# Column sums of the modulation vectors in a two-block transformer kernel: ones products replaced by transposes and ScalarE sums

## The chip, the core and the metric

The kernel runs on one core of a Trainium2 chip. The core has a matrix engine (TensorE, PE in the profile, with its weight loads shown apart as PEld), two engines that work on 128 partitions at once (VectorE, DVE; ScalarE, ACT), GpSimd (POOL) and SyncE (SP), which here only issue transfers, and 16 DMA engines. The metric is the time of one execution on the device in microseconds (us). The kernel before takes 2347.35 us, the median of three runs (2347.17 to 2348.92).

## What is computed

Two transformer blocks follow each other on 256 rows of 2048 columns, all in float32. What matters here is the second block's modulation: two vectors of 2048 values (one for the rows, one for the context) go through a SiLU and a 2048 x 12288 matrix, and the six resulting vectors (shifts SH1 and SH2, scales SC1 and SC2, gates GT1 and GT2) modulate the normalised rows.

```python
mx = jax.nn.silu(c) @ w_mod[i] + b_mod[i]
mc = jax.nn.silu(c_ctx) @ w_mod[i] + b_mod[i]
sh1, sc1, gt1, sh2, sc2, gt2 = [t[:, None, :] for t in jnp.split(mx, 6, axis=-1)]
sh1c, sc1c, gt1c, sh2c, sc2c, gt2c = jnp.split(mc, 6, axis=-1)
hc = modulate(rmsnorm(ctx, norm1_g[i]), sh1c, sc1c)      # h * (1 + scale) + shift
hx = modulate(rmsnorm(x, norm1_g[i]), sh1, sc1)
```

Of the context's six vectors only SH1 and SC1 are needed.

## The kernel before

**The large products.** Every weight matrix is read in groups of 512 rows x 512 columns (1 MB, two pieces of 256 rows). For each piece ScalarE rounds the float32 weights to a short form (`whi`, L486, `round_groups`), VectorE forms the remainder (`wlo`, L919, `remainders`), and TensorE multiplies three times: short times short, remainder times short, short times remainder (L1516 to L1518, `multiply`). A group is 24 products of 128x512. `whi` and `wlo` hold two groups, so ScalarE and VectorE work two groups ahead of TensorE: ScalarE rounds a piece of group g+2 as soon as TensorE has finished that piece of group g (semaphore `piece_multiplied`), VectorE follows it (`hi_done`), TensorE waits for `lo_done`. The product of four groups stands in one of two pairs of PSUM banks and is then taken out by ScalarE (`proj`, L595; `relu_square`) or added to the rows by VectorE (`add_block`, L1124).

**The modulation beside them.** The matrix `w_mod` is not multiplied on TensorE. GpSimd loads it in 192 steps of 256 rows x 512 columns into the two slots of `mring`, and VectorE adds the rows, each scaled by its value of `csil`, into `macc` (`mod_steps`, L935 and L939), two instructions of 128x512 a step, or four where the context is wanted too ("dual": SH1, SC1). After eight steps `macc` holds, for 512 columns, 128 partial sums, one in each partition. TensorE sums them over the partitions (`reduce_mod`, L1541): one product per 128 columns with `macc` as weights and a column of ones, four for a single vector, eight for a dual one, into `m1`. VectorE then adds the bias and writes `modT` (`set_mod`, L948), and only after that starts the next eight steps, which overwrite `macc`.

**When.** There are 24 such reductions: four of SH1 (dual) beside the first block's input projection and the start of its output projection; in each of the four chunks of the first block's MLP (32 groups, `mlp_chunk`) one of SC2, SC1 (dual), GT1 and SH2, after groups 7, 15, 22 and 30 (`MLP_REDUCED`); and four of GT2 in the second block's input projection (`in_blocks`). The order on each engine is the order in which its code is written; loops over chunks and pairs of blocks repeat it.

**Other users of the banks.** `m0` also takes the unused output of ScalarE's squares (`square`, L520), from which the norms come. At the end of a chunk VectorE adds block 3 (L1124, `h_added`), and ScalarE squares it; in the first chunk ScalarE squares the context instead, and both engines then scale it (L1006 to L1020, L549).

Of the kernel before, what the change touches and what calls it, by code (L numbers as in the profile page):

```python
# [108 lines left out]
def two_blocks(nc, x, ctx_in, w_in, w_fourier, w_out, w_up, w_down, w_mod, w_in2, w_out2, w_gate,  # L109
               w_up2, w_down2, vectors, gates_w, mid_g, final_g, tables, fourier_tables, attn_tables, out):  # L110
    ctx = ExitStack()
    with ctx:
# [24 lines left out]
        modT = sb("modT", [P, 2, 6 * KT])  # L137
        gain1 = sb("gain1", [P, 2, KT])
# [78 lines left out]
        mod_reduced = sem("mod_reduced")  # L217
        mod_set = sem("mod_set")
# [257 lines left out]
        def _(act):  # L476
# [37 lines left out]

            def square(src, col, piece, junk=m0):

                for t in range(T):
                    if c.n.get("ssq", 0):
                        act.wait_ge(ssq_done, c.at("ssq"))
                    act.activation(junk[:, :], src[:, t, bass.ds(col, NB)], ACT.Square,  # L520
                                   accum_out=squares[:, t, bass.ds(piece, 1)]).then_inc(ssq_done, 1)
                    c.add("ssq")
# [55 lines left out]
            def w_in_pair(i, first=False):  # L578
                for j in range(2):
# [17 lines left out]
                    last.then_inc(proj_set, 1)  # L597

# [6 lines left out]
            with c.loop(act, 4, 1, g=8) as i:  # L605
# [55 lines left out]
            for n in range(3):  # L661
                round_groups(4)
# [27 lines left out]
            def mlp_chunk(first=False, last=False):  # L690

                def round_group(g):
                    round_groups(1)
                    if last and g in CTX_TURNS:
# [20 lines left out]
            with c.loop(act, MLP_CHUNKS - 1, 1, g=32, q=8, half=4, blk=4, ha=4, ssq=4 * T):  # L715
# [193 lines left out]
        def _(dve):  # L909
# [33 lines left out]

            def set_mod(kind, i, dual):

                dve.wait_ge(mod_reduced, c.at("mb", 1))
                for who in range(2 if dual else 1):
                    dve.tensor_tensor(modT[:, who, bass.ds(i * 4 + kind * KT, 4)], m1[:, 4 * who:4 * who + 4],  # L948
                                      vecs[:, 1, bass.ds(i * 4 + kind * KT, 4)], ALU.add).then_inc(mod_set, 1)
# [89 lines left out]
            def w_in_pair(i, first=False):  # L1039

                for g in range(8):
# [10 lines left out]
                    elif not first and g == 1:  # L1052
                        mod_steps(1, 7, True)
                        remainders(1)
                        set_mod(SH1, i - 1, True)
                    elif g != 1:
                        remainders(1)
                    if g >= 2:
# [15 lines left out]
            with c.loop(dve, 4, 1, g=8, m=8, ma=32, mb=1) as i:  # L1074
# [45 lines left out]
            set_mod(SH1, 3, True)  # L1120
# [11 lines left out]
            for n in range(4):  # L1132
# [6 lines left out]
                remainders(1)  # L1139
            remain_added(3)  # L1140
# [11 lines left out]
            def mlp_chunk(i, first=False, last=False):  # L1152
                done = 0
                for g in range(32):
# [9 lines left out]
                    if g in MLP_REDUCED:  # L1164
                        set_mod(MLP_REDUCED[g], i, MLP_REDUCED[g] == SC1)
                        if last and MLP_REDUCED[g] == SC1:
# [19 lines left out]
            with c.loop(dve, MLP_CHUNKS - 1, 1, g=32, q=8, hi=8, m=32, ma=80, mb=4) as i:  # L1186
# [107 lines left out]
            def in_blocks(names, p):  # L1294
                for n, name in enumerate(names):
                    following = (names + (("w_out",) if p else ("cc0",)))[n + 1]
                    which, part = MOD_PAIRS[p].get(name, (None, 0))
                    for kg in range(2 if name == "l" else 4):
# [7 lines left out]
                        if which is not None:  # L1306
                            k = 4 * part + kg
                            mod_steps(SPREAD[k], sum(SPREAD[0:k]), False)
                            if k == 7:
                                set_mod(GT2, which, False)  # L1310
# [684 lines left out]
```

## Time and profile before

| what | value |
|---|---|
| three runs, median (lowest to highest) | 2347.35 us (2347.17 to 2348.92) |
| the profiled execution's own time | 2348.28 us |
| its span in the profile | 2346.6 us |
| TensorE busy | 2301.8 us, 98% |
| VectorE, ScalarE busy | 1552.7 us, 1082.0 us |
| moved by DMA | 523.92 MB, mean 223 GB/s |

The profile is of one execution. Times in its rows are counted from the start of the span; "x8" in a row of the timeline means eight instructions that follow each other, with the time from the first one's start to the last one's end. Matrix products overlap, so what one costs is read from the distance between starts, not from its duration. What stands in brackets at a row's end is the idle time of that engine before it and what ended it. A float32 product with ones is recorded as two passes, a transpose and a product of the large matrices as one.

### The profile page before, as it was taken

How to read it: one execution, taken by the hardware profiler on the slowest of the kernel's cores; microseconds unless marked ns; L12 is line 12 of the kernel's file. 1: busy time of each engine (PE TensorE's matmuls, PEld its weight loads, DVE VectorE, ACT ScalarE, POOL GpSimd, SP SyncE). 2: the span in 40 equal slices, each digit the busy share in tenths (PEclk: the TensorE clock that was granted, in tenths of full speed). 3: DMA queues.
4: the chain of work that ended last, by engine and by line, in shares of the span. 5: the costliest groups of instructions: out<-in, count | busy, mean ns of one | idle time of the engine just before them, and what ended most of it. 6: DMA issues, size and time to landing. Idle time of an engine off the chain costs nothing.

```text
span 2346.6 us, 29309 instructions
## 1 busy us (share of the span) xinstructions
PE 2301.8 (98%) x10637; PEld 1894.0 (81%) x10637; DVE 1552.7 (66%) x1845; ACT 1082.0 (46%) x1295; POOL 146.2 (6%) x213
## 2 busy tenths in 40 slices
PE   8999999999999999999999999998999999999997
PEld 7887888888888888888877877787888888888886
DVE  7987558877877877886778664466445544555545
ACT  5445455445444444445463464444444344434444
POOL 1110001111111111110010000000000000000000
PEclk9999999999999999999999999999999999999999
DMA  9884459888887888886677663464555665555553
GB/s 343 292 273 148 128 177 312 294 290 286 269 292 259 267 299 267 269 277 213 224 246 217 202 215 117 154 233 154 187 191 186 208 200 185 196 189 190 196 179 108
DMA packets 245187, 523.92 MB, mean 223 GB/s; under 512 B 20016, under 2 KB 20288, under 8 KB 243776
## 3 DMA queue, kind: packets, MB, share of 16 engines
q1 hardware_dynamic: 213680, 404.80, 52.8%
q0 software_dynamic: 29568, 111.97, 13.8%
q10 hardware_dynamic: 1808, 5.37, 0.6%
q8 instruction: 86, 1.41, 0.2%
q14 instruction: 45, 0.37, 0.0%
HBM read 517.87 MB, written 4.21 MB: 222 GB/s over the span
## 4 chain that ended last, share of the span: by engine, by line
PE 96%; DVE 2%; ACT 1%; issue 1%; DMA 0%; ACTq 0%; DVEq 0%
PE acc L1516 30%; PE acc L1518 29%; PE acc L1517 29%; PE tp L1531 2%; PE m L1541 1%; PE tp L1806 1%; DVE wlo L919 0%; PE acc L1651 0%; PE m L1772 0%; PE tp L1824 0%; PE tp L1818 0%; PE acc L1615 0%; PE tp L1751 0%; PE tp L1762 0%; PE m L1625 0%
## 5 line engine op out<-in xcount | busy, mean ns | idle before, releaser
L919 DVE TENSOR_TENSOR wlo<-wring,whi 128x1024 fp32r<-128x1024 f32 x776 | 935.2, 1214 | 602.7 <-ACT whi L486 599.3
L486 ACT ACTIVATE whi<-wring 128x1024 fp32r<-128x1024 f32 x776 | 813.5, 1051 | 1115.5 <-PE acc L1518 1112.0
L1516 PE MATMUL acc<-whi,xhi 128*128 128x512 f32 x2112 | 833.7, 395 | 2.7 <-issue 1.9
L1518 PE MATMUL acc<-whi,xlo 128*128 128x512 f32 x2112 | 823.9, 390 | 0.0
L1517 PE MATMUL acc<-wlo,xhi 128*128 128x512 f32 x2112 | 823.4, 390 | 0.0
L1516 PEld LDWEIGHTS acc<-whi,xhi 128*128 128x128 f32 x2112 | 397.5, 188 | 95.3 <-issue 14.4
L1518 PEld LDWEIGHTS acc<-whi,xlo 128*128 128x128 f32 x2112 | 397.2, 188 | 84.1
L1517 PEld LDWEIGHTS acc<-wlo,xhi 128*128 128x128 f32 x2112 | 397.8, 188 | 81.0 <-issue 0.7
L939 DVE SCALAR_TENSOR_TENSOR macc<-mring,csil,macc 128x512 f32<-128x512 f32 x480 | 344.2, 747 | 28.0 <-DMA mring<-w_mod 21.2
L1516 PE MATMUL acc<-whi,ahi 128*128 128x512 f32 x608 | 239.1, 393 | 2.6 <-DVE h L1124 1.4
L1518 PE MATMUL acc<-whi,alo 128*128 128x512 f32 x608 | 237.0, 390 | 0.0
L1517 PE MATMUL acc<-wlo,ahi 128*128 128x512 f32 x608 | 236.6, 389 | 0.0
L425 POOL DMA_DIRECT2D mring<-w_mod x192 | 136.4, 711 | 1125.4 <-DVE macc L939 1104.5
L1516 PE MATMUL acc<-whi,bhi 128*128 128x512 f32 x352 | 137.2, 390 | 1.6 <-DVE blo L959 1.6
L1517 PE MATMUL acc<-wlo,bhi 128*128 128x512 f32 x352 | 137.0, 389 | 0.0
L1518 PE MATMUL acc<-whi,blo 128*128 128x512 f32 x352 | 137.0, 389 | 0.0
L1516 PEld LDWEIGHTS acc<-whi,ahi 128*128 128x128 f32 x608 | 114.2, 188 | 26.2 <-issue 3.3
L1518 PEld LDWEIGHTS acc<-whi,alo 128*128 128x128 f32 x608 | 114.1, 188 | 24.2
L1517 PEld LDWEIGHTS acc<-wlo,ahi 128*128 128x128 f32 x608 | 114.2, 188 | 23.0
L1516 PEld LDWEIGHTS acc<-whi,bhi 128*128 128x128 f32 x352 | 66.1, 188 | 15.5 <-DVE blo L959 1.8
L1518 PEld LDWEIGHTS acc<-whi,blo 128*128 128x128 f32 x352 | 66.1, 188 | 13.8
L1517 PEld LDWEIGHTS acc<-wlo,bhi 128*128 128x128 f32 x352 | 66.1, 188 | 13.5
(213 smaller groups left out, 1047.6 us busy)
## 6 DMA issues: line engine op xcount, KB each, us to landing
wring<-w_up SPq DMA_DIRECT2D x216, 512.0 KB, 4.7
wring<-w_down SPq DMA_DIRECT2D x216, 512.0 KB, 5.0
mring<-w_mod POOLq DMA_DIRECT2D x192, 512.0 KB, 5.1
wring<-w_in SPq DMA_DIRECT2D x184, 512.0 KB, 5.5
wring<-w_gate SPq DMA_DIRECT2D x88, 512.0 KB, 4.4
wring<-w_out SPq DMA_DIRECT2D x64, 512.0 KB, 4.8
gbig<-ctx_in POOLq DMA_DIRECT2D x2, 1024.0 KB, 8.5
hspill<-h ACTq DMA_DIRECT2D x1, 2048.0 KB, 7.9
```

What stands on the lines that cost most here:

```text
L425: pool.dma_start(mring[:, c.slot("m", MSLOTS), :, :], w_mod_v[s, :, :, bass.ds(i * NB + kind * D, NB)])\
L486: act.activation(whi[:, piece_slot(c, piece), 0:half], wring[:, g4, piece * half:(piece + 1) * half], ACT.Copy).then_inc(hi_done, 1)
L919: dve.tensor_tensor(wlo[:, h4, 0:half], wring[:, g4, piece * half:(piece + 1) * half], whi[:, h4, 0:half].bitcast(F32), ALU.subtract).then ...
L939: dve.scalar_tensor_tensor(macc[:, who, :], mring[:, m2, kt, :], csil[:, who, k:k + 1], macc[:, who, :], ALU.mult, ALU.add).then_inc(mod_a ...
L1516: pe.matmul(dst, hi[:, tile, rows], whi[:, h4, w], start=(kg == first and k == 0), stop=False)
L1517: pe.matmul(dst, hi[:, tile, rows], wlo[:, h4, w], start=False, stop=False)
L1518: last = pe.matmul(dst, lo[:, tile, rows], whi[:, h4, w], start=False, stop=(kg == final and k == KG - 1))
L1531: last = pe.transpose(tp[:, q, j * S + t * P:j * S + (t + 1) * P], src[:, t, f:f + P], ident)
L1541: last = pe.matmul(m1[:, 4 * who + j:4 * who + j + 1], macc[:, who, j * P:(j + 1) * P], ones[:, 0:1], start=True, stop=True)
L1806: last = pe.matmul(tp[:, (q + bank) % 2, (ck // 2) * DV:(ck // 2 + 1) * DV], kdec[rows, ck // 2, d, hd * DK:(hd + 1) * DK], gv[rows, ck // ...
```

## The change

In 20 of the 24 reductions (SH1, SC2, SC1, GT1, SH2) TensorE no longer multiplies with ones. It transposes each 128x128 part of `macc` against the identity into a bank: `m1` for the rows' vector, `m0` for the context's. ScalarE then reads each 128 columns of the bank, writes them back in place with Copy, and sums them in its accumulator into one column of `modsum` (`sum_mod`). VectorE waits for the transposes before it overwrites `macc` (`take_mod`), and adds the bias from `modsum` one group later (`set_mod`). ScalarE's `square` waits for its own sums, since both write `m0`. The four reductions of GT2 stay as they were, under the names `reduce_gate` and `set_gate`. The tables, the transfers and GpSimd's and SyncE's order are the same.

```diff
@@ tiles and semaphores @@
+        modsum = sb("modsum", [P, 2, KG])
...
+        mod_turned = sem("mod_turned")
+        mod_summed = sem("mod_summed")
@@ ScalarE @@
+            def sum_mod(dual):
+
+                for who in range(2 if dual else 1):
+                    bank = m0 if who else m1
+                    c.add("mt")
+                    act.wait_ge(mod_turned, c.at("mt"))
+                    for j in range(KG):
+                        cols = slice(j * P, (j + 1) * P)
+                        act.activation(bank[:, cols], bank[:, cols], ACT.Copy,
+                                       accum_out=modsum[:, who, j:j + 1]).then_inc(mod_summed, 1)
+
             def square(src, col, piece, junk=m0):
...
+                    if t == 0 and c.n.get("mt", 0):
+                        act.wait_ge(mod_summed, c.at("mt", 0, KG))
...
                     last.then_inc(proj_set, 1)
+                    if not first and j == 0:
+                        sum_mod(True)
...
             for n in range(3):
-                round_groups(4)
+                round_groups(2)
+                if n == 0:
+                    sum_mod(True)
+                round_groups(2)
                 round_added(n)
...
                 def round_group(g):
                     round_groups(1)
+                    if g - 1 in MLP_REDUCED:
+                        sum_mod(MLP_REDUCED[g - 1] == SC1)
@@ VectorE @@
+            def take_mod(dual):
+
+                c.add("mt", 2 if dual else 1)
+                dve.wait_ge(mod_turned, c.at("mt"))
+
             def set_mod(kind, i, dual):
 
+                c.add("msum", KG * (2 if dual else 1))
+                dve.wait_ge(mod_summed, c.at("msum"))
+                for who in range(2 if dual else 1):
+                    dve.tensor_tensor(modT[:, who, bass.ds(i * 4 + kind * KT, 4)], modsum[:, who, :],
+                                      vecs[:, 1, bass.ds(i * 4 + kind * KT, 4)], ALU.add).then_inc(mod_set, 1)
+
+            def set_gate(kind, i):
+
                 dve.wait_ge(mod_reduced, c.at("mb", 1))
-                for who in range(2 if dual else 1):
-                    dve.tensor_tensor(modT[:, who, bass.ds(i * 4 + kind * KT, 4)], m1[:, 4 * who:4 * who + 4],
-                                      vecs[:, 1, bass.ds(i * 4 + kind * KT, 4)], ALU.add).then_inc(mod_set, 1)
+                dve.tensor_tensor(modT[:, 0, bass.ds(i * 4 + kind * KT, 4)], m1[:, 0:4],
+                                  vecs[:, 1, bass.ds(i * 4 + kind * KT, 4)], ALU.add).then_inc(mod_set, 1)
                 c.add("mb")
...
                         mod_steps(1, 7, True)
                         remainders(1)
-                        set_mod(SH1, i - 1, True)
                     elif g != 1:
                         remainders(1)
+                    if not first and g == 2:
+                        take_mod(True)
+                    elif not first and g == 3:
+                        set_mod(SH1, i - 1, True)
                     if g >= 2:
                         mod_steps(1, g - 2, True)
...
-            set_mod(SH1, 3, True)
...
                 add_block(n * NB, n % 2)
                 remainders(1)
+                if n == 0:
+                    take_mod(True)
+                    set_mod(SH1, 3, True)
...
                     if g in MLP_REDUCED:
-                        set_mod(MLP_REDUCED[g], i, MLP_REDUCED[g] == SC1)
-                        if last and MLP_REDUCED[g] == SC1:
+                        take_mod(MLP_REDUCED[g] == SC1)
+                    if g - 1 in MLP_REDUCED:
+                        kind = MLP_REDUCED[g - 1]
+                        set_mod(kind, i, kind == SC1)
+                        if last and kind == SC1:
                             set_gain1()
...
-                                set_mod(GT2, which, False)
+                                set_gate(GT2, which)
@@ TensorE @@
                 pe.wait_ge(mod_acc, c.at("ma", 8))
                 for who in range(2 if dual else 1):
+                    bank = m0 if who else m1
                     for j in range(4):
-                        last = pe.matmul(m1[:, 4 * who + j:4 * who + j + 1], macc[:, who, j * P:(j + 1) * P],
-                                         ones[:, 0:1], start=True, stop=True)
+                        last = pe.transpose(bank[:, j * P:(j + 1) * P], macc[:, who, j * P:(j + 1) * P], ident)
+                    last.then_inc(mod_turned, 1)
+
+            def reduce_gate(per_nb):
+
+                c.add("ma", per_nb)
+                pe.wait_ge(mod_acc, c.at("ma", 8))
+                for j in range(4):
+                    last = pe.matmul(m1[:, j:j + 1], macc[:, 0, j * P:(j + 1) * P], ones[:, 0:1], start=True, stop=True)
                 last.then_inc(mod_reduced, 1)
...
-                        reduce_mod(16, False)
+                        reduce_gate(16)
```

On VectorE, in the loop over pairs of blocks of the input projection, before (L919 makes a remainder `wlo`, L948 writes `modT`):

```order
L919 TENSOR_TENSOR wlo<-wring,whi 128x1024 [waits hi_done]
L918 REGISTER_ALU
L919 TENSOR_TENSOR wlo<-wring,whi 128x1024 [waits hi_done]
L948 ISA [waits mod_reduced]
L948 REGISTER_ALU
L948 TENSOR_TENSOR modT<-m,vecs 128x4
L948 ISA
L948 TENSOR_TENSOR modT<-m,vecs 128x4
L918 REGISTER_ALU
L919 TENSOR_TENSOR wlo<-wring,whi 128x1024 [waits hi_done]
L918 REGISTER_ALU
L919 TENSOR_TENSOR wlo<-wring,whi 128x1024 [waits hi_done]
```

and now (L942 makes a remainder, L962 adds into `macc`, L977 writes `modT`):

```order
L962 SCALAR_TENSOR_TENSOR macc<-mring,csil,macc 128x512 [waits mod_acc]
L941 REGISTER_ALU
L942 TENSOR_TENSOR wlo<-wring,whi 128x1024 [waits hi_done]
L941 REGISTER_ALU
L942 TENSOR_TENSOR wlo<-wring,whi 128x1024 [waits hi_done]
L975 REGISTER_ALU
L977 ISA [waits mod_summed]
L977 REGISTER_ALU
L977 TENSOR_TENSOR modT<-modsum,vecs 128x4
L977 ISA
L977 TENSOR_TENSOR modT<-modsum,vecs 128x4
```

The write of `modT` has moved behind the remainders of one more group, the first step of the next sum (the L962 row at the top is its last instruction) and the remainders of a second group, and waits for ScalarE's sums; ahead of that first step stands a wait for TensorE's transposes (`mod_turned`).

On ScalarE, in the same loop, the two copies of a finished block (`proj`) and the rounding of the next weights (`whi`), before:

```order
L595 ISA [waits piece_multiplied]
L595 ACTIVATE proj<-acc,rstd 128x512
L595 ISA
L595 ACTIVATE proj<-acc,rstd 128x512
L485 REGISTER_ALU [waits piece_landed2_0]
L486 ACTIVATE whi<-wring 128x1024 [waits piece_multiplied]
L485 REGISTER_ALU [waits piece_landed2_1]
```

and now (L526 is a sum):

```order
L611 ISA [waits piece_multiplied]
L611 ACTIVATE proj<-acc,rstd 128x512
L611 ISA
L611 ACTIVATE proj<-acc,rstd 128x512
L523 ISA
L526 ACTIVATE m,modsum<-m 128x128 [waits mod_turned]
L526 ACTIVATE m,modsum<-m 128x128 x3
L526 ACTIVATE m,modsum<-m 128x128 [waits mod_turned]
L526 ACTIVATE m,modsum<-m 128x128 x3
L488 REGISTER_ALU [waits piece_landed2_0]
L489 ACTIVATE whi<-wring 128x1024 [waits piece_multiplied]
```

Eight sums now stand between the copies and the next rounding.

On VectorE at the end of the MLP's first chunk, before (L1124 adds the last block, L1006 to L1020 are the context's norm):

```order
L919 TENSOR_TENSOR wlo<-wring,whi 128x1024 [waits hi_done] x2
L948 TENSOR_TENSOR modT<-m,vecs 128x4 [waits mod_reduced]
L1124 TENSOR_TENSOR h<-acc,h 128x2x512 [waits piece_multiplied]
L919 TENSOR_TENSOR wlo<-wring,whi 128x1024 [waits hi_done] x2
L1006 TENSOR_REDUCE ssq<-squares 128x2 [waits ssq_done]
L1008 TENSOR_SCALAR ssq<-ssq 128x2 [waits squares_summed]
L1014 RECIPROCAL rstd<-ssq 128x2 [waits root_done]
L1020 TENSOR_SCALAR gbig<-gbig,rstd 128x2048 [waits rstd_done]
```

and now:

```order
L942 TENSOR_TENSOR wlo<-wring,whi 128x1024 [waits hi_done] x2
L977 TENSOR_TENSOR modT<-modsum,vecs 128x4 [waits mod_summed,mod_turned]
L1161 TENSOR_TENSOR h<-acc,h 128x2x512 [waits piece_multiplied]
L942 TENSOR_TENSOR wlo<-wring,whi 128x1024 [waits hi_done] x2
L1041 TENSOR_REDUCE ssq<-squares 128x2 [waits ssq_done]
L1043 TENSOR_SCALAR ssq<-ssq 128x2 [waits squares_summed]
L1049 RECIPROCAL rstd<-ssq 128x2 [waits root_done]
L1055 TENSOR_SCALAR gbig<-gbig,rstd 128x2048 [waits rstd_done]
```

No row has moved here; what the write of `modT` waits for has changed. Before it waited for products that TensorE had issued a group earlier, now for sums that ScalarE makes at this place, and the addition of the last block and the remainders of the next group stand behind it.

## Rows read from the trace of the kernel before

**Rows 1.** The page: TensorE's busy time, the chain that ended last, ScalarE's rounding
```profile
PE 2301.8 (98%) x10637; PEld 1894.0 (81%) x10637; DVE 1552.7 (66%) x1845; ACT 1082.0 (46%) x1295; POOL 146.2 (6%) x213
...
PE 96%; DVE 2%; ACT 1%; issue 1%; DMA 0%; ACTq 0%; DVEq 0%
...
L486 ACT ACTIVATE whi<-wring 128x1024 fp32r<-128x1024 f32 x776 | 813.5, 1051 | 1115.5 <-PE acc L1518 1112.0
```

**Rows 2.** Timeline (start us, duration us, engine): first products of two successive groups, TensorE
```profile
889.44 0.39 PE L1516 MATMUL acc<-whi,ahi 128*128 128x512 f32 x1
...
894.88 0.39 PE L1516 MATMUL acc<-whi,ahi 128*128 128x512 f32 x1
```

**Rows 3.** TensorE timeline: a dual reduction, then a single one, between products
```profile
121.55 0.39 PE L1518 MATMUL acc<-whi,xlo 128*128 128x512 f32 x1
121.78 1.84 PE L1541 MATMUL m<-ones,macc 128*128 128x1 f32 x16
123.48 0.49 PE L1516 MATMUL acc<-whi,xhi 128*128 128x512 f32 x1
...
384.74 0.39 PE L1518 MATMUL acc<-whi,alo 128*128 128x512 f32 x1
...
385.78 0.49 PE L1516 MATMUL acc<-whi,ahi 128*128 128x512 f32 x1
```

**Rows 4.** TensorE timeline: eight transposes, then four, between products
```profile
372.94 0.40 PE L1518 MATMUL acc<-whi,alo 128*128 128x512 f32 x1
373.17 1.04 PE L1531 MATMUL tp<-tabs,blk 128*128 128x128 f32 x8
373.96 0.47 PE L1516 MATMUL acc<-whi,ahi 128*128 128x512 f32 x1
...
1009.85 0.40 PE L1518 MATMUL acc<-whi,xlo 128*128 128x512 f32 x1
...
1010.44 0.48 PE L1516 MATMUL acc<-whi,xhi 128*128 128x512 f32 x1
```

**Rows 5.** The products with ones by form: busy us, mean ns, idle before
```profile
L1541 PE MATMUL m<-ones,macc 128*128 128x1 f32 x256 | 30.0, 242 | 0.0
```

**Rows 6.** ScalarE timeline: accumulating ACTIVATEs and what starts behind them
```profile
1421.57 0.38 ACT L791 ACTIVATE tmpT<-tp 128x256 f32<-128x256 f32 x1
...
1421.93 0.39 ACT L790 ACTIVATE h<-tp 128x256 f32<-128x256 f32 x1
...
890.98 0.60 ACT L520 ACTIVATE m<-h 128x512 f32<-128x512 f32 x1 [0.28 <-DVE h L1124]
...
891.74 0.60 ACT L520 ACTIVATE m<-h 128x512 f32<-128x512 f32 x1
```

**Rows 7.** Timelines of VectorE, ScalarE, TensorE behind the second SH1 reduction
```profile
123.88 0.30 DVE L948 TENSOR_TENSOR modT<-m,vecs 128x4 f32 x2 [2.45 <-PE m L1541]
130.36 1.23 DVE L919 TENSOR_TENSOR wlo<-wring,whi 128x1024 fp32r<-128x1024 f32 x1 [0.62 <-ACT whi L486]
131.50 2.73 DVE L939 SCALAR_TENSOR_TENSOR macc<-mring,csil,macc 128x512 f32<-128x512 f32 x4
...
130.23 1.25 ACT L595 ACTIVATE proj<-acc,rstd 128x512 f32 x2
...
139.94 0.39 PE L1516 MATMUL acc<-whi,xhi 128*128 128x512 f32 x1
```

**Rows 8.** ScalarE and VectorE timelines at the end of the third chunk
```profile
889.64 1.06 ACT L486 ACTIVATE whi<-wring 128x1024 fp32r<-128x1024 f32 x1 [1.66 <-PE acc L1518]
...
889.64 1.23 DVE L1124 TENSOR_TENSOR h<-acc,h 128x1024 f32<-128x1024 f32 x1 [4.01 <-PE acc L1518]
890.78 2.35 DVE L919 TENSOR_TENSOR wlo<-wring,whi 128x1024 fp32r<-128x1024 f32 x2
```

**Rows 9.** Timelines at the end of the first chunk: VectorE, then TensorE
```profile
523.14 1.22 DVE L1124 TENSOR_TENSOR h<-acc,h 128x1024 f32<-128x1024 f32 x1 [3.95 <-PE acc L1518]
530.36 2.36 DVE L919 TENSOR_TENSOR wlo<-wring,whi 128x1024 fp32r<-128x1024 f32 x2 [1.70 <-ACT whi L486]
...
533.82 0.39 PE L1516 MATMUL acc<-whi,ahi 128*128 128x512 f32 x1
```

**Rows 10.** Busy us of each engine in a window, granted clock of TensorE (PEclk)
```profile
372.00:376.00 4.00, 4.00 (x23) 3.37 (x22) 3.39 (x5) 2.03 (x3) 1.26 (x2) 1.00 0.81 250
1500.00:1503.50 3.50, 3.50 (x10) 2.79 (x9) 2.23 (x8) 1.32 (x3) 0.00 (x0) 0.54 0.05 16
```

More of the change, by code:

```diff
@@ L604, in _ @@
             w_in_pair(0, True)
-            with c.loop(act, 4, 1, g=8) as i:
+            with c.loop(act, 4, 1, g=8, mt=2) as i:
                 w_in_pair(i)
@@ L714, in _ @@
             root_and_scale(2, u_g, u_g)
-            with c.loop(act, MLP_CHUNKS - 1, 1, g=32, q=8, half=4, blk=4, ha=4, ssq=4 * T):
+            with c.loop(act, MLP_CHUNKS - 1, 1, g=32, q=8, half=4, blk=4, ha=4, ssq=4 * T, mt=5):
                 mlp_chunk()
@@ L1073, in _ @@
             w_in_pair(0, True)
-            with c.loop(dve, 4, 1, g=8, m=8, ma=32, mb=1) as i:
+            with c.loop(dve, 4, 1, g=8, m=8, ma=32, mt=2, msum=2 * KG) as i:
                 w_in_pair(i)
@@ L1185, in _ @@
             norm_scale(2, u_g, u_g)
-            with c.loop(dve, MLP_CHUNKS - 1, 1, g=32, q=8, hi=8, m=32, ma=80, mb=4) as i:
+            with c.loop(dve, MLP_CHUNKS - 1, 1, g=32, q=8, hi=8, m=32, ma=80, mt=5, msum=5 * KG) as i:
                 mlp_chunk(i)
```

## The prediction

> **What bounds the kernel now.** I read the page's busy line first, then its chain of waits: TensorE is busy 98% of the span and holds 96% of the chain, DMA none of it [rows 1]. The question to each engine is then for whom it waits: ScalarE's rounding sat idle 1115.5 us, 1112.0 of them for TensorE's products [rows 1]. So the other engines follow TensorE, and time comes or goes in two ways: instructions on TensorE change, or an engine that supplies it comes too late. For both I read the timeline. TensorE's unit is the distance between starts: 24 products of a group from 889.44 to 894.88, 0.227 us each, 5.44 a group [rows 2]; a duration of 0.39 counts the overlap too.
>
> **TensorE's own part.** What a reduction costs is the distance from the last product before it to the first one behind it, less one ordinary distance.
> - Dual, eight products with ones: 123.48 - 121.55 - 0.23 = 1.70 us; single, four: 385.78 - 384.74 - 0.23 = 0.81 us [rows 3].
> - Eight transposes: 373.96 - 372.94 - 0.23 = 0.79 us; four: 1010.44 - 1009.85 - 0.23 = 0.36 us [rows 4].
>
> The trace of before has no transpose of `macc`, but these have its shape, type and identity operand, and change only the source. A product with ones is recorded as two passes: 256 records are 128 products, 8 x 8 + 12 x 4 = 112 in the reductions that change and 16 in GT2's, which stay [rows 5]. A dual reduction gives back 0.91 us, a single one 0.45: 8 x 0.91 + 12 x 0.45 = 12.7 us. TensorE's order is otherwise the same, so nothing else is removed or added there.
>
> That a transpose costs its distance and not its duration is seen in the same rows: four more of them add (0.79 - 0.36) / 4 = 0.11 us each, and eight take 1.04 us from first start to last end, so one alone lasts 1.04 - 7 x 0.11 = 0.27 [rows 4]. The Trainium skill (TensorE: Matmul & The Clock Gate, Part 4: PE-mode transpose) gives about 275 ns for one inside a kernel; the trace agrees with that as a duration and disagrees with it as a price.
>
> **The sums on ScalarE.** New are 112 ACTIVATEs of 128x128 with the reading of the accumulator, in lots of eight (dual) or four. None of this shape is in the trace. Nearest is one of 128x256 from PSUM, also accumulating: the next instruction starts 1.93 - 1.57 = 0.36 us behind it [rows 6]. From 256 to 512 columns the duration grows from 0.38 to 0.60, 0.86 ns a column [rows 6], so 128 columns less are 0.11 less: **0.25 us** a sum. The other bound is the square of 128x512, which waits each time for the one before: 0.76 us to the next [rows 6], less 384 x 0.86 ns = 0.43 us. I take 0.25, since the sums wait for nothing in between; even the whole 0.76 is kept as the far end. Below 0.25 nothing would be gained, since the sums reach the end of the kernel only through others' waits. In all 112 x 0.25 = 28 us on an engine that is idle for half the span; what counts is where they stand.
>
> **Where VectorE now waits for them.** `set_mod` waits for the sums, and remainders that TensorE needs stand behind it. Three places.
> - Projection (SH1, three times). ScalarE's copies start at 130.23 and take 1.25, then eight sums: 131.5 + 2.0 + 0.2 for the last reading = 133.7. VectorE is free from 130.36 + 1.23 = 131.6 and waits 2.1 us. Then the two writes 0.3, a step 2.73, the next remainder 1.23: 138.0; TensorE wants it at 139.94 [rows 7]. Slack 2.0 us, so nothing is lost until a sum costs 0.50. In exchange the wait of 2.45 us for the ones products goes [rows 7]. A group costs VectorE 2 x 1.23 + 2.73 = 5.2 us here against 5.44 on TensorE, so a lag is made up slowly, but it is made up.
> - End of an MLP chunk (SH2, four times). ScalarE rounds from 889.64 to 890.7, sums until 890.7 + 1.0 + 0.1 = 891.8; VectorE, which added the last block at 889.64, does it now from 892.0, behind its write of 0.15. It ends at 893.2, the first remainder 1.2 later at 894.4; TensorE wants it at 894.88 [rows 2, 8]. Slack 0.5 us, gone when a sum costs 0.37.
> - The first chunk's end in particular. There the norm and the scaling stand behind it, so all of the shift of 2.3 us (889.64 to 892.0) reaches the remainder that now starts at 530.36 and is done 1.2 later, at 531.5. 533.9 against TensorE's 533.82 [rows 9]: 0.1, with the reload of weights 0.2 us lost.
>
> The other sums (SC2, SC1, GT1, and SH1's last, beside the output projection) stand behind a rounding in the middle of a chunk or block; VectorE waits 0.5 to 2.1 us there while it is two groups, 10.9 us, ahead, and SC1's dual sums are followed by single steps of half the length. I put them at nothing. `take_mod` waits for transposes that TensorE issues straight after a group whose release VectorE's own remainders wait for, so it is met when reached; its cover is one rounding and one remainder, 1.06 + 1.23 us [rows 7, 8], against 0.79. `square` waits for sums directly ahead of it on its own engine: under 0.2 us each. GpSimd's loads follow VectorE's steps and lie up to 2 us later or earlier; no queue holds anything else behind them there.
>
> **Sum.** 12.7 - 0.2 = 12.5 us. The profiled execution took 2348.28 us (span 2346.6), so the changed kernel's would take 2335.8. That execution lies 0.9 above the median of the three runs; from the median, 2347.35 - 12.5 = **2334.9 us**.
>
> **The rivals.**
> - A sum costs 0.43 us, not 0.25: for it speaks the square; against it, that the square's price holds a wait for itself. Chunk ends are then 0.7 later: three lose 0.2, the first 0.9; the projection keeps 0.6. Gain 12.7 - 1.5 = 11.2: 2336.2, and up to 2341 where a sum comes to 0.6.
> - The gain is given back: a sum costs the full 0.76. Then the projection loses 8 x (0.76 - 0.50) = 2.1 three times, three chunk ends 4 x (0.76 - 0.37) = 1.6, the first 0.2 + 4 x 0.51 = 2.2: 13.3 lost against 12.7, 2348. Against it: four times the columns cost that.
> - Slower, by the same mechanism at the same places: each further 0.1 us a sum costs 3 x 0.8 + 4 x 0.4 = 4.0 us. From about 0.86 us the kernel is more than 4.7 us slower; at 1.0 us, 2357.6. For it: reading and writing the same columns of one bank with the accumulator is nowhere in the trace. Against: nothing of half this length takes so long.
> - Slower, by the clock: transposes could count as idleness, and the granted clock fall to its lower level, 1.2 GHz, behind each reduction. After TensorE had idled, the window from 1500 has 0.54 granted and 10 products in 3.5 us [rows 10], 3.5 - 10 x 0.227 = 1.2 us lost. Twenty times that is 25 us: 2360. Against it: the window with eight transposes, 372 to 376, has 1.00 [rows 10]. The Trainium skill (TensorE: Matmul & The Clock Gate, Part 4: PE-mode transpose) says that transposes do not count as work for the clock as products do; by that rule alone this rival would be likelier, and the trace at 372 gives no sign of it.
>
> - Slower, because the transposes don't overlap: then eight cost 8 x 0.27 = 2.2 us against 1.70 and four 1.1 against 0.81, 8 x 0.5 + 12 x 0.29 = 7.5 us more than before: 2355. Against it: all transposes of this kernel that follow each other overlap, as in rows 4, whatever their source.
>
> **Chances.** Forecast 0.68, dearer sums 0.17, given back 0.08, slower by the sums 0.04, by the clock 0.02, by transposes in single file 0.01. Anything within 0.2% (4.7 us) is no change that a measurement tells. Faster by more: 0.86; within: 0.08; slower: 0.06. The range: below, the forecast with all sums hidden and one low-clock stretch fewer, 2347.35 - 12.7 - 1.2 = 2333.4, and 0.6 for the runs' own spread; above, the dearer sums up to 0.6 us: 2332.8 to 2341.
>
> **What would show it.** Eight transposes of `macc` with 0.8 us between products, four with 0.36; starts of ScalarE's sums 0.25 apart; VectorE's write of `modT` idle ahead for about 2 us in the projection, released by ScalarE, and nowhere a product of TensorE idle behind it but perhaps at the first chunk's end. It is wrong if sums start more than 0.4 apart, if TensorE's first product behind a chunk's end shows a wait for `wlo`, or if the granted clock falls before 1500.

## The result, and the profile after

The changed kernel takes **2357.64 us** (median of six runs, 2356.82 to 2358.99) against 2347.26 us for the kernel before (six runs, 2346.53 to 2348.92): ratio 1.0045, 95% interval 1.0035 to 1.0055. It is 10.4 us slower where 12.5 us faster was forecast. The span of the profiled execution grew from 2346.6 to 2357.3 us.

The page of the changed kernel: busy times, the chain by engine, the groups with `ahi` and `bhi`, and for comparison one with `xhi`. (Line, operation, operands, count; busy us, mean ns; idle us before and its releaser.)
```profile
PE 2309.3 (98%) x10525; PEld 1882.9 (80%) x10525; DVE 1551.6 (66%) x1845; ACT 1111.9 (47%) x1519; POOL 146.6 (6%) x213
...
PE 94%; DVE 3%; ACT 1%; issue 1%; DMA 0%; DVEq 0%; ACTq 0%; POOLq 0%
...
L1559 PE MATMUL acc<-whi,xhi 128*128 128x512 f32 x2112 | 832.2, 394 | 2.7 <-issue 1.9
...
L1559 PE MATMUL acc<-whi,ahi 128*128 128x512 f32 x608 | 243.3, 400 | 1.0 <-DVE wlo L942 1.0
...
L1559 PE MATMUL acc<-whi,bhi 128*128 128x512 f32 x352 | 139.5, 396 | 1.6 <-DVE blo L994 1.6
```
The same groups on the page of before:
```profile
L1516 PE MATMUL acc<-whi,xhi 128*128 128x512 f32 x2112 | 833.7, 395 | 2.7 <-issue 1.9 <-DVE wlo L919 0.6
...
L1516 PE MATMUL acc<-whi,ahi 128*128 128x512 f32 x608 | 239.1, 393 | 2.6 <-DVE h L1124 1.4 <-DVE wlo L919 1.2
...
L1516 PE MATMUL acc<-whi,bhi 128*128 128x512 f32 x352 | 137.2, 390 | 1.6 <-DVE blo L959 1.6
```
TensorE has 112 instructions fewer than in [rows 1] (10637 to 10525) and is busy 7.5 us longer. The products' groups on the two pages say where: products that load `ahi` or `bhi` are longer (393 to 400 ns with `ahi`, 390 to 396 ns with `bhi`), those with `xhi` are not. The change touches none of them.

TensorE's timeline of the changed kernel (start us, duration us): a dual reduction, a single one, and the first products of two successive groups with `ahi`, which answer to [rows 3] and [rows 2].
```profile
120.33 0.40 PE L1561 MATMUL acc<-whi,xlo 128*128 128x512 f32 x1
120.56 1.04 PE L1585 MATMUL m<-tabs,macc 128*128 128x128 f32 x8
121.36 0.47 PE L1559 MATMUL acc<-whi,xhi 128*128 128x512 f32 x1
...
385.46 0.39 PE L1561 MATMUL acc<-whi,alo 128*128 128x512 f32 x1
385.69 0.60 PE L1585 MATMUL m<-tabs,macc 128*128 128x128 f32 x4
386.04 0.48 PE L1559 MATMUL acc<-whi,ahi 128*128 128x512 f32 x1
...
892.82 0.39 PE L1559 MATMUL acc<-whi,ahi 128*128 128x512 f32 x1
...
898.41 0.40 PE L1559 MATMUL acc<-whi,ahi 128*128 128x512 f32 x1
```
The reductions cost what was forecast: 121.36 - 120.33 - 0.23 = 0.80 us for a dual, 386.04 - 385.46 - 0.23 = 0.35 us for a single one. But a group of 24 products with `ahi` takes 898.41 - 892.82 = 5.59 us, not 5.44 [rows 2]. Over all products, the mean distance between starts is 233.1 to 233.4 ns where `ahi`, `alo`, `bhi` or `blo` is loaded (below: the a products) and 227.0 to 227.3 ns with `xhi` or `xlo` (the x products); in the kernel before all kinds have 226.6 to 227.5.

ScalarE's timeline of the changed kernel, behind the first SH1 reduction in the loop:
```profile
84.78 0.28 ACT L526 ACTIVATE m<-m 128x128 f32<-128x128 f32 x1
84.98 0.19 ACT L526 ACTIVATION_READ_ACCUMULATOR m<-m 128x1 f32 x1
85.06 0.27 ACT L526 ACTIVATE m<-m 128x128 f32<-128x128 f32 x1
```
A sum costs 85.06 - 84.78 = 0.28 us, not 0.25.

Aligned product by product (there are 9216 of 512 columns in both), the two profiles differ as follows, in us:

| where | after against before |
|---|---|
| 8 dual and 12 single reductions | -12.7 |
| 2880 a products, 6 ns each | +17.6 |
| the first two heads (196 to 246 us) | +3.6 |
| back edge of the MLP's loop (705 to 715 us) | +3.7 |
| a reduction that waits for `macc` at 1026.84 | +0.9 |
| the low-clock stretch at 1500 [rows 10], not there | -2 |
| sum; spans | +11.1; +10.7 |

The row on the stretch at 1500 is no gain of the change: of the kernels below, five with the old reductions lack that stretch too (e3, e7, e9, e10 and e12), and three with the new ones have it (e1, e6 and e11).

Two of these are waits. VectorE's timeline of the changed kernel: `modT`'s write in the projection, and the last projection step with the first head's scores.
```profile
87.42 0.30 DVE L977 TENSOR_TENSOR modT<-modsum,vecs 128x4 f32 x2 [2.43 <-ACT m L526]
...
196.23 2.72 DVE L962 SCALAR_TENSOR_TENSOR macc<-mring,csil,macc 128x512 f32<-128x512 f32 x4
198.88 0.67 DVE L1123 SCALAR_TENSOR_TENSOR blk<-tab_a,acc 128x512 f32<-128x512 f32 x1
```
TensorE's timeline of the changed kernel, the scores of the first two heads:
```profile
196.11 1.13 PE L1666 MATMUL acc<-qkT 128*128 128x256 f32 x4 [0.63 <-ACT qkT L641]
...
201.81 1.25 PE L1666 MATMUL acc<-qkT 128*128 128x256 f32 x4 [2.35 <-ACT qkT L641]
```
and of before:
```profile
199.21 1.13 PE L1615 MATMUL acc<-qkT 128*128 128x256 f32 x4 [0.63 <-ACT qkT L623]
...
204.21 1.13 PE L1615 MATMUL acc<-qkT 128*128 128x256 f32 x4 [1.65 <-ACT qkT L623]
```
VectorE's timeline of before, the first head's scores:
```profile
201.28 0.68 DVE L1085 SCALAR_TENSOR_TENSOR blk<-tab_a,acc 128x512 f32<-128x512 f32 x1
```
No product in the projection is late. But VectorE arrives at the heads later against TensorE: it reads the first scores 198.88 - 196.11 = 2.77 us behind the start of their products, where before it was 201.28 - 199.21 = 2.07 us, and TensorE waits 2.35 us for the second head instead of 1.65. Then the clock falls. Windows of the changed kernel (busy us of each engine; PEclk is the granted clock):
```profile
120.00:124.00 4.00, 4.00 (x24) 3.35 (x23) 4.00 (x6) 1.06 (x1) 0.43 (x1) 1.00 0.60 162
...
202.50:209.30 6.80, 6.11 (x25) 5.07 (x24) 3.96 (x13) 2.54 (x6) 0.00 (x0) 0.51 0.18 74
706.50:709.90 3.40, 0.11 (x1) 0.00 (x0) 2.33 (x3) 1.67 (x10) 0.00 (x0) 1.00 0.22 81
711.00:714.50 3.50, 3.50 (x10) 2.72 (x10) 1.40 (x2) 1.06 (x1) 0.00 (x0) 0.54 0.55 156
```
Around a dual reduction (120 to 124) 1.00 is granted; 0.51, the level of 1.2 GHz, stands behind the wait at the second head, and 0.54 behind 3.4 us at 706.5 in which TensorE ran nothing.

### The profile page after: what moved, and what is told of

It is laid out like the page before. It is cut to its first block, busy times and chain, and to the rows that moved or that the text cites. A ratio compares the mean times of both kernels' runs of the same rounds, so it can differ in the third digit from the quotient of the medians.

```text
span 2357.3 us, 29359 instructions
## 1 busy us (share of the span) xinstructions
PE 2309.3 (98%) x10525; PEld 1882.9 (80%) x10525; DVE 1551.6 (66%) x1845; ACT 1111.9 (47%) x1519; POOL 146.6 (6%) x213
## 4 chain that ended last, share of the span: by engine, by line
PE 94%; DVE 3%; ACT 1%; issue 1%; DMA 0%; DVEq 0%; ACTq 0%; POOLq 0%
PE acc L1559 29%; PE acc L1561 29%; PE acc L1560 29%; PE tp L1574 2%; DVE wlo L942 1%; PE tp L1857 1%; DVE macc L962 1%; PE m L1585 1%; PE acc L1702 0%; ACT whi L489 0%; PE m L1823 0%; PE tp L1875 0%; PE tp L1869 0%; PE tp L1802 0%; PE tp L1813 0%
## 5 line engine op out<-in xcount | busy, mean ns | idle before, releaser
L942 DVE TENSOR_TENSOR wlo<-wring,whi 128x1024 fp32r<-128x1024 f32 x776 | 933.2, 1213 | 596.7 <-ACT whi L489 593.3
L962 DVE SCALAR_TENSOR_TENSOR macc<-mring,csil,macc 128x512 f32<-128x512 f32 x480 | 344.3, 747 | 34.0 <-DMA mring<-w_mod 26.7
```

Of the source, the lines that this page charges most:

```text
L942: dve.tensor_tensor(wlo[:, h4, 0:half], wring[:, g4, piece * half:(piece + 1) * half], whi[:, h4, 0:half].bitcast(F32), ALU.subtract).then ...
L962: dve.scalar_tensor_tensor(macc[:, who, :], mring[:, m2, kt, :], csil[:, who, k:k + 1], macc[:, who, :], ALU.mult, ALU.add).then_inc(mod_a ...
```

## The experiments

**What is common to them.** `modsum` is declared in the middle of the list of tiles. It takes 32 bytes of each partition, and all tiles behind it move by 32: `ahi` and `bhi` from address 163712 to 163744, `alo` and `blo` from 180096 to 180128. `whi` (49280), `wlo` (65664), `xhi` (110720) and `xlo` (127104) stand ahead of it and stay. In a product the a or x tile is the operand that is loaded (128 columns), `whi` or `wlo` the one that is streamed (512). The first four kernels ask whether that shift is the 17.6 us.

**e1: the change with every tile at its old place.**
```diff
-        modsum = sb("modsum", [P, 2, KG])
+        modsum = vrows[:, 0, 0:2 * KG].rearrange("p (w k) -> p w k", w=2)
```


> The changed kernel with modsum put into vrows, whose contents are used up at the start, so that no other tile moves from where it lay before the change. Theory 1 (placement: the products whose weights come from ahi, alo, bhi or blo are slower because the new tile of 32 bytes has moved these tiles by 32 bytes): distances of 0.227 us everywhere again, 17.6 us back, about 2340, and 2335 to 2336 if the two losses at the attention heads (3.6 us) and behind the MLP loop's first round (3.7 us) go with it. Theory 2 (the sums on ScalarE or the transposes slow the products, whatever the places): distances of 0.233 us as in the changed kernel, 2357 to 2358.

Measured: 2340.33 us (ten runs) against 2346.37, ratio 0.9976 (0.9967 to 0.9985). All products are 227 ns apart again. The change itself is faster, but by 6 us and not by 12.5.

**e2: the kernel before with 32 bytes ahead of `gain1`, nothing else.**
```diff
+        sb("pad", [P, 8])
         gain1 = sb("gain1", [P, 2, KT])
```


> The kernel before with an unused tile of 32 bytes where the change puts modsum, and nothing else. Theory 1: the products with weights from ahi, alo, bhi, blo stand 0.233 us apart, 2816 of them x 6.3 ns = 17.6 us slower: 2365. Theory 2: no change, 2347.

Measured: 2365.67 us, ratio 1.0080 (1.0066 to 1.0094); a products 233.1 to 233.5 ns apart, x products 227.0 to 227.2. A tile that nobody reads costs 19 us.

**e3 and e4: which tile, and which multiple?** e3 moves `xhi` and `xlo` by 32 bytes and the a tiles by 64, e4 `whi` and `wlo` by 32 and all behind them by 64; in both `oss` and `orstd` lie in used rows of `vrows` and make room. The pads of e3 (in e4 they stand around `whi` and `wlo`):
```diff
+        sb("pad_a", [P, 8])
         xhi = sb("xhi", [P, KT, S], F32R)
         xlo = sb("xlo", [P, KT, S], F32R)
+        sb("pad_b", [P, 8])
```


> The kernel before with xhi and xlo moved by 32 bytes and all tiles behind them by 64 (oss and orstd lie in vrows to make room). Theory 1, where what counts is that the weights operand starts at a multiple of 64 bytes: products with xhi and xlo 6.3 ns slower, 6150 x 6.3 ns = 39 us, those with ahi, alo, bhi, blo unchanged at 0.227: 2386. If a multiple of 128 bytes is wanted, both kinds are slower: 2403. If it is something of ahi and bhi alone (their neighbours, their place in memory): 2347.

> The kernel before with whi and wlo, the operand that streams through, moved by 32 bytes and all tiles behind them by 64. If the loss is in loading the weights operand: no change, 2347. If it is in the streamed operand as well: up to all 9216 products x 6.3 ns = 58 us slower, 2405; ScalarE and VectorE, which write these tiles, may take longer, which would show in their durations (1.06 and 1.22 us).

Measured: 2402.09 us, ratio 1.0237 (1.0221 to 1.0253), and 2401.21 us, 1.0229 (1.0211 to 1.0248); one of e4's four executions took 4729.65 us, unexplained, and is left out of the ratio; the other three took 2400.56 to 2401.81. In both kernels all kinds of products are 233.0 to 233.5 ns apart. At that point "the loaded operand wants a multiple of 128 bytes" fitted everything: the x, a and w tiles of before all lie on one.

**e5: the streamed operand by itself.**
```diff
+        ssq = sb("ssq", [P, 7, T])
         whi = sb("whi", [P, HSLOTS, HALF * NB], F32R)
         wlo = sb("wlo", [P, HSLOTS, HALF * NB], F32R)
+        rstd = sb("rstd", [P, 7, T])
```


> The kernel before, with ssq declared ahead of whi and rstd ahead of mring (no tile is added): whi and wlo, the operand that TensorE streams in the 512-wide products, lie 64 bytes further (off a multiple of 128 bytes), and all that follows up to squares lies 128 bytes further; xhi, xlo, ahi, alo, bhi and blo, the weights operands, stay on multiples of 128 bytes. Theory 1 (only the place of the weights operand counts): products stay 227 ns apart and the time is that of the kernel before, 2346 to 2348 us. Rival (the streamed operand's place counts too, which the run with both moved could not tell apart, since its weights operands lay 64 bytes off as well): all 9216 products 233 ns apart, 2346 + 9216 x 0.006 = about 2401 us; a third way, both operands count half each, would be about 2374 us.

Measured: 2389.79 us, ratio 1.0179 (1.0163 to 1.0194), which is none of the three. The x products are 233.3 ns apart though `xhi` is on a multiple of 128, the a products, whose loaded tile did not move, 227.7 to 230.6. So my rule fell; three others were left.

**e7 to e10: place or distance?** The next four move the tiles so that the rules part. e7 declares `csil` (128 bytes) ahead of `whi`; e8 declares it ahead of `xhi`, with `gain1` in a used row of `vrows`; e10 declares `csil` and `gain1` ahead of `xhi`, with `modT` in used rows of `vrows` and a pad in its place. e9 is one line:
```diff
+        sb("pad", [P, 8])
         whi = sb("whi", [P, HSLOTS, HALF * NB], F32R)
```


> The kernel before with csil declared ahead of whi: whi, wlo (w) and xhi, xlo (x) lie 128 bytes further, ahi, alo, bhi, blo (a) stay. In the run with w +64 and x +128 the products with x were 233.3 ns apart and those with a 228 to 231, which 'each on a multiple of 128' leaves open (x was on one). Theory M (each operand wants a multiple of 128): 227 ns everywhere, 2347 us. Rival Q (each wants the same place within 256 bytes as before): products with x 233 or more, with a as in that run 228 to 231 or 233: 2347 + 6336 x 0.006 + 2880 x 0.003 = about 2394 us. Rival D (what counts is the distance between the two operands' places): x 227, a 233: 2347 + 2880 x 0.006 = about 2364 us.

> The kernel before with csil ahead of xhi and gain1 in a used row of vrows: w at its place, x 128 bytes further, a 128 bytes nearer. Theory M: 227 ns everywhere, 2347 us. Rivals Q and D (place within 256 bytes, or distance modulo 256): all products 233 ns apart, 2347 + 9216 x 0.006 = about 2402 us.

> The kernel before with a pad of 32 bytes ahead of whi: w, x and a all 32 bytes further, their distances as before. Theory M and rival Q: all products off their place, 233 ns apart, about 2402 us. Rival D (only the distance counts): 227 ns everywhere, 2347 us.

> The kernel before with w at its place, x 256 bytes further and a 256 bytes nearer (csil and gain1 ahead of xhi, modT in used rows of vrows with a pad in its stead). Theory M, and rivals Q and D with a period of 256 bytes: 227 ns everywhere, 2347 us. If 233 ns are seen for one or both, the period is longer, or it is not a matter of the address modulo a power of two.

Measured: e7 2362.01 us (three runs), ratio 1.0063 (1.0040 to 1.0086); e8 2395.86 (two runs), 1.0208 (1.0178 to 1.0238); e9 2346.92, 0.9999 (0.9988 to 1.0011); e10 2347.25, 1.0006 (0.9995 to 1.0017). The products' groups on e7's page:
```profile
L1516 PE MATMUL acc<-whi,xhi 128*128 128x512 f32 x2112 | 833.2, 395 | 2.7 <-issue 1.9 <-DVE wlo L919 0.6
...
L1516 PE MATMUL acc<-whi,ahi 128*128 128x512 f32 x608 | 241.9, 398 | 2.2 <-DVE wlo L919 1.2 <-issue 1.0
```
and on e9's:
```profile
L1517 PE MATMUL acc<-whi,xhi 128*128 128x512 f32 x2112 | 833.0, 394 | 2.7 <-issue 1.9 <-DVE wlo L920 0.6
...
L1517 PE MATMUL acc<-whi,ahi 128*128 128x512 f32 x608 | 239.0, 393 | 2.3 <-DVE wlo L920 1.2 <-issue 1.1
```
In e7 the tiles that moved (w and x, together) are fast and the one that stayed is slow. In e9 all of TensorE's large tiles have moved off every multiple of 64 bytes and nothing is slow. The distance between the two operands' tiles decides, and a whole 256 bytes more or less in it change nothing (e10). All runs together:

| distance of the loaded tile from the streamed one, modulo 256 bytes | ns between starts | seen in |
|---|---|---|
| 0 | 226.5 to 227.5 | before, e1, e6, e9 to e12; x in after, e2, e7 |
| 32 | 233.0 to 233.5 | a in after, e2; x in e3; all in e4 |
| 64 | 233.2 to 233.5 | a in e3, x in e5 |
| 128 | 232.2 to 232.6 | a in e7, x and a in e8 |
| 192 | 227.7 to 230.6 | a in e5 |

The row of 192 rests on one kernel, and why it is milder than 64 no run shows.

**e11: the change word for word, its new tile declared elsewhere.**
```diff
+        modsum = sb("modsum", [P, 2, KG])
         whi = sb("whi", [P, HSLOTS, HALF * NB], F32R)
```


> The change word for word, but modsum is declared ahead of whi, so that all tiles from whi on lie 32 bytes further and the distances between them are those of before. Theory D (the distance between TensorE's two operands counts, not their place): products 227 ns apart everywhere; the time is that of the change with all places kept, 2340.3 us, between 2338.5 and 2342 with the loop's back edge. Rival (the new tile's cost has to do with the sums' own accesses, or with places): 233 ns with a alone or with all, 2357 or about 2395 us.

Measured: 2340.76 us, ratio 0.9975 (0.9963 to 0.9986), products 226.5 to 227.3 ns apart in all kinds. This is the same finding from the other side: one declaration moved takes the loss away, with all of TensorE's tiles at other addresses than before.

**e6: and the waits?** Against before, e1's profile still loses 2.1 us at the heads, 2.6 at the loop's edge, 1.0 at the reduction that waits for `macc` and 0.4 at the first chunk's end. These 6.1 us are most of what lies between the 12.7 us of the reductions and the 6 us measured. Here `set_mod` moves behind work that needs no sums.
```diff
-                    elif not first and g == 3:
+                    elif not first and g == 5:
                         set_mod(SH1, i - 1, True)
...
-                    if g - 1 in MLP_REDUCED:
-                        kind = MLP_REDUCED[g - 1]
-                        set_mod(kind, i, kind == SC1)
...
                     if g == 31:
                         remainders(1)
+                    if g - 1 in MLP_REDUCED:
+                        kind = MLP_REDUCED[g - 1]
+                        set_mod(kind, i, kind == SC1)
```


> The change with every tile at its place of before (the sums lie in the used row 0 of vrows), and VectorE takes the sums later: in the projection behind group 5's remainders instead of group 3's, in the MLP at the end of the group in which it stood at the start, behind the modulation steps and the block's addition. TensorE's and ScalarE's instructions are those of the run with all places kept (2340.3 us). Theory: VectorE's waits for ScalarE's sums (2.43 us in each projection pair) go, so at the heads its step ends 0.3 us or more earlier, TensorE's extra wait there and the half clock behind it go (2.1 us), as do the 0.4 us at the first chunk's end; the loop's back edge (2.6 + 1.0 us) stays: 2340.3 - 2.1 - 0.4 = about 2337.8 us, and 2337 if the extra 0.9 us at 1015 us go too. Rival (the waits were slack, and the clock falls at the heads without them): 2340 us, no change against the run with all places kept; a second rival (VectorE's work that now stands ahead of the sums only moves the wait to ScalarE or TensorE a group later): 2341 to 2343 us.

Measured: 2338.31 us (2336.20 to 2340.41) against 2346.98, ratio 0.9958 (0.9945 to 0.9972); the profiled execution is the slowest of the five. TensorE's timeline of e6, the heads and the loop's edge:
```profile
200.70 1.13 PE L1666 MATMUL acc<-qkT 128*128 128x256 f32 x4 [1.65 <-ACT qkT L641]
...
695.99 0.39 PE L1561 MATMUL acc<-whi,xlo 128*128 128x512 f32 x1
696.49 0.49 PE L1559 MATMUL acc<-whi,ahi 128*128 128x512 f32 x1
...
697.52 0.40 PE L1560 MATMUL acc<-wlo,ahi 128*128 128x512 f32 x1
...
701.75 0.59 PE L1561 MATMUL acc<-whi,alo 128*128 128x512 f32 x1 [3.84 <-issue]
702.14 0.63 PE L1559 MATMUL acc<-whi,ahi 128*128 128x512 f32 x1
702.57 0.63 PE L1560 MATMUL acc<-wlo,ahi 128*128 128x512 f32 x1
```
Windows of e6, at the heads and behind the edge:
```profile
200.00:212.00 12.00, 9.93 (x62) 8.64 (x63) 7.36 (x23) 6.55 (x18) 0.00 (x0) 1.00 0.19 67
...
702.00:707.00 5.00, 5.00 (x13) 3.84 (x13) 0.97 (x1) 1.06 (x1) 0.00 (x0) 0.51 0.52 195
```
The heads are as before: wait 1.65, clock 1.00. This is shown, then: VectorE's lag from the projection made both the longer wait and the half clock there. The extra at the reduction that waits for `macc` only fell from 1.0 (e1) to 0.8 us, and a new one of 0.4 us came at the reduction at 833.58. The edge is most of what e6 still lacks: it gained 7.9 us of span (2346.6 to 2338.7) and lost 5.1 at the edge, more than e1's 2.6, so its profiled span is no shorter than e1's (2338.4). Against before, e6's and e1's ratios overlap (0.9945 to 0.9972 and 0.9967 to 0.9985): that the heads' loss is gone is read from the trace, and the 2 us between the two medians are not clear of noise.

**e12: is the edge ScalarE's?** At the back edge (group 112) kernels with the old reductions stand still for up to 1.6 us, as before does:
```profile
705.09 0.39 PE L1518 MATMUL acc<-whi,xlo 128*128 128x512 f32 x1
706.90 0.49 PE L1516 MATMUL acc<-whi,ahi 128*128 128x512 f32 x1 [1.42 <-DVE h L1124]
```
The releaser named is not to be trusted: in e6 the same addition runs from 696.41 to 697.64, and TensorE starts its next product at 696.49, so it doesn't wait for it. VectorE's timeline of e6:
```profile
696.41 1.23 DVE L1161 TENSOR_TENSOR h<-acc,h 128x1024 f32<-128x1024 f32 x1 [3.61 <-PE acc L1561]
```
e12 adds activations that nobody reads to ScalarE's loop (`scrap` stands ahead of `whi`, as the pad in e9):
```diff
+                    if g - 1 in MLP_REDUCED:
+                        act.wait_ge(scrap_done, c.at("sc"))
+                        for k in range(8 if MLP_REDUCED[g - 1] == SC1 else 4):
+                            act.activation(scrap[:, k:k + 1], vecs[:, 2, k:k + 1], ACT.Copy).then_inc(scrap_done, 1)
+                            c.add("sc")
```


> The kernel before with all 32 bytes further, and in each MLP chunk 20 activations of one column on ScalarE where the change has its 20 sums; they are read by nobody. TensorE's and VectorE's work is that of before. At the back edge of the MLP's loop (about 705 us) TensorE stood still for 0 to 1.6 us in ten profiles of kernels with the old reductions and for 2.6 to 4.0 us in the three with the new ones, whose TensorE program is of the same length at every point. Theory E (ScalarE's longer loop body holds the edge up): 2.6 us or more here, 2347 + 1 to 4 = 2348 to 2351 us. Rival (it has to do with TensorE's or VectorE's side of the change, or with chance): 0 to 1.6 us here, 2347 us.

Measured: 2345.95 us, ratio 0.9997 (0.9987 to 1.0007); 1.0 us at the edge. 20 more activations a chunk on ScalarE don't do it. This is not the whole of the change's lengthening: a sum is recorded as two instructions, so the change adds 40 a chunk (ScalarE's instructions go from 1295 to 1375 in e12 and to 1519 in the changed kernel). In all, the edge's gaps sum to 0 to 1.6 us in the ten profiles with the old reductions, and to 2.6 (e1), 3.6 (after), 4.2 (e11) and 4.3 (e6) in the four with the new ones, the long one always behind five products of the new group and put down to "issue".

What causes it stays open, but the traces have a candidate. TensorE's program is not of the same length, as the expectation above says: with the new reductions it has 104 fewer recorded instructions ahead of the loop and 1726 instead of 1766 in each pass through it (a product with ones is recorded as two products and two weight loads, a transpose as one of each). And the packets of the queue that moves instructions (q8; packets, MB, share of 16 engines' time) come otherwise. Up to the new group's first product, before (700 to 706.9 us):
```profile
q8 instruction: 2, 0.03, 3.4%
```
In the changed kernel, from 700 us to the fifth product (706.3), and in the gap behind it (706.3 to 709.9):
```profile
q8 instruction: 1, 0.02, 1.3%
...
q8 instruction: 1, 0.02, 1.6%
```
In each of the ten profiles with the old reductions two such packets come in the 15 us ahead of the first product, the later one ending 1.7 to 2.3 us before it. In each of the four with the new ones only one comes there, the next one comes in the gap, and the sixth product starts 1.4 to 1.6 us behind its end. A TensorE that waits for its own instructions would fit all fourteen. But the trace does not say whose instructions q8 carries, and no run varied it: this is argued, not shown, and VectorE's part was not tried either.

## Why the prediction was wrong

- **The step that failed: "TensorE's order is otherwise the same, so nothing else is removed or added there."** The order is the same, but the declaration of a tile belongs to the change as well. It put 32 bytes between the places of the operands of 2880 products, 2880 x 6.1 ns = 17.6 us. e2 has that alone (19 us), e1 and e11 the change without it (6 us and 6.6 us faster). None of the rivals contained it, and the range, 2332.8 to 2341.0, had no room for it. Without it the kernel lands inside the range (2340.3 and 2340.8), at its upper end, and that is luck: the upper part stood for sums of 0.43 to 0.6 us, which did not come, and was filled by the heads, the loop's edge and a late `macc`. It is luck too that a slower rival named 2357.6: it asked for sums of 1.0 us.
- **TensorE's own part: right.** 1.70 to 0.80 and 0.81 to 0.35 us a reduction, 12.7 us in sum. e6's profile is 13.0 us shorter outside the loop's edge, which holds small differences of both signs as well.
- **The clock rival: right to put it low.** No reduction is followed by the lower level. The Trainium skill (TensorE: Matmul & The Clock Gate, Part 4: PE-mode transpose) does not count transposes as work for the clock. No run here tests that: each lot, of 0.80 us at most, stands between products. But the clock did fall earlier than 1500, as the prediction's last sentence asked, behind waits of TensorE (0.51 at the heads, 0.54 at the loop's edge).
- **The sums: nearly right.** 0.28 us for 0.25, so the rivals that lived on 0.43 and more are out.
- **"Slack 2.0 us, so nothing is lost": wrong in what it looked at.** The wait was 2.43 us, not 2.1, and TensorE's products of the projection did not wait, as said. The lag was not made up before the heads, though, where VectorE is in TensorE's path: 0.7 us more wait, and with the half clock 3.6 us. In e1 it was 2.1: the wait was no shorter, 2.48 us, but the half clock lasted 3.4 us instead of 6.8. I had measured the slack against the next product and not against the end of the stage.
- **The chunk ends: right.** VectorE waits 6 us there for the sums, and no product there waits for `wlo` (the page's 1.0 us stands at 1109.21, behind the MLP, and was 1.2 before); the first chunk's end lost 0.4 us (e1) against 0.2.
- **The other sums, put at nothing: nearly.** At the last chunk's GT1 reduction `macc` came late, 0.9 us (1.0 in e1).
- **The loop's edge: not foreseen**, 2.0 us more of gap (1.0 in e1, 2.7 in e6) and then about 1.5 at half clock (2.4 in e6). "Nothing else is removed or added there" left out here too that TensorE's recorded instructions became fewer; whether that is the cause is not settled.

## What to carry to other kernels

A new tile is an edit to every tile declared behind it. Before a change is judged, compare the addresses of TensorE's two operands with those of the kernel before; put new small tiles where no distance between operands changes, and let a kernel that only adds the padding run beside it. Measure slack to the point where the late engine next stands in the path, which may be in the next stage: here 2.4 us of "harmless" waiting came back as 3.6.

The fastest version measured is e6, 2338.3 us, 0.42% faster than the kernel before (0.28 to 0.55%): the change, every tile in its place, and the sums taken later. Its lead over e1 is within the noise.

## What the runs showed of the hardware

- The rate of these back-to-back 128x512 products (float32 bits rounded to `fp32r`, 128x128 weights) depends on how far the loaded operand's tile lies from the streamed one's, modulo 256 bytes: 227 ns at 0, 232 to 233 at 32, 64 and 128, 228 to 231 at 192. Other distances were not tried. Where each lies by itself makes no difference (e9). The Trainium skill (TensorE: Matmul & The Clock Gate, Part 2: What happens when you issue a matmul, "Step-by-step: what each phase is for") says that weights have a read port of their own and that loading them takes no SBUF bandwidth from the running product. By that, where the two tiles lie to each other should not matter, and in these runs it does: with the distance at 32 for all 9216 products the kernel is 55 us slower (e4, 2401.2 against 2346.4), with all tiles moved but the distances kept not at all (e9). That the two reads meet in some part of the memory is my reading of it; no run shows where.
- Transposes of `macc` cost 0.11 us each in a lot, as those of other tiles [rows 4].
- An accumulating ACTIVATE of 128x128 in PSUM, with its reading, costs 0.28 us from start to start.
- At the second head TensorE ran at half clock behind an idle stretch of 2.35 us (for 6.8 us, granted clock 0.51), but not behind one of 1.65 us at the same place (before, e6; granted clock 1.00 in e6).
